# Attention stage of a two-layer trunk: causal mask by a TensorE product, one minimum and one transposed copy per pair

## The chip, the cores and the metric

The kernel runs on one core of one Trainium2 chip. The metric is the device time of one launch in microseconds, of which each kernel has several runs; a profiled execution gives the trace. TensorE multiplies matrices into PSUM (eight banks of 512 float32 per partition), VectorE, ScalarE and GpSimd (POOL in the profile) work on rows of 128 partitions, and SyncE issues transfers. Each engine works its own list of instructions in order, and engines meet by semaphores that the kernel sets and waits for by hand.

## The reference, cut to what matters

The trunk has two layers, each with a mixer (a recurrent unit, six heads of latent attention, six heads of sparse attention) and a channel mixer (dense in the first layer, eight experts in the second), on 512 tokens of 1024 numbers. The change touches attention alone. What its pairs of heads compute is a causal softmax over 512 keys (with 512 tokens the selected blocks and the window of the sparse attention are all keys up to the query):

```python
def masked_softmax(s, mask):
    s = jnp.where(mask, s, NEG_INF)
    m = jnp.max(s, axis=-1, keepdims=True)
    e = jnp.where(mask, jnp.exp(s - m), 0.0)
    return e / jnp.maximum(jnp.sum(e, axis=-1, keepdims=True), 1e-30)

        s = jnp.einsum('bqhd,bkhd->bhqk', qi, k).astype(jnp.float32) * scale
        p = masked_softmax(s, (kpos[None, :] <= qpos[:, None])[None, None])
        return jnp.einsum('bhqk,bkhd->bqhd', p.astype(v.dtype), v)
...
        out = gt[..., 0:1] * o_c + gt[..., 1:2] * o_s + gt[..., 2:3] * o_w
```

`o_c` is attention over 31 compressed keys, computed ahead of the stage; `o_s` and `o_w` are the selected and the window branch, and `gt` are the gates of a head.

## The kernel before

Per layer there is a long preparation (input projections, rotary turns, norms, written out step by step in the list `PREPARE`), then the attention stage, then the output projection and the channel mixer. The attention stage works through nine pairs of heads, `PAIRS`: six sparse ones (three pairs of heads, each for branch 1 and 2, kind `nsa`, with 64 rows of keys per head) and three latent ones (kind `mla`, 96 rows). Each pair is cut into four query blocks of 128 (`TT` = 4). One iteration g is a pair u and a block i = g mod 4, with (i + 1) x 128 keys; there are `ND` = 36 iterations. The two heads of a pair are `ab` = 0 and 1, and an item is n = 2g + ab.

The order is written by hand, as one loop per engine over g, with fixed distances:

- TensorE: `scores(g)` (two float32 products into two of four score banks; in sparse pairs the heads sit in rows 0 to 63 and 64 to 127), then `turn(g-3)` (float32 transposes of 128x128 blocks of the weights, head 0 into bank 4, head 1 into bank 5), then `values` of the pair before: for key block kb the products of all queries from block kb on. The first value step of a sparse branch 1 also multiplies the compressed weights (line 1376). In the first iterations `spare` products on the identity `identb` (line 423) fill TensorE.
- VectorE: `maximum(2g)`, `maximum(2g+1)` (line 2111: adds the mask `causal`, negates, writes the block back to PSUM and takes the minimum into `nmx`), then `scale(g-2)` (sum, for sparse pairs times the reciprocal of the gate, then reciprocal) and two `scaled` (line 2134: the weights times the factor of each row). Steps of the recurrent unit (`lru_finish`) are laid into g = 14 to 21, and `collect` takes a finished pair out of PSUM.
- ScalarE: `exps(g)` (line 1657: two exps with the sum of each row), then `turned(g-3)` (line 1668: one copy for each head of the transposed blocks to `PT_`).

So one pass of an item is: scores, maximum, exp, scaling, transposes, copy, value products. `scores` waits for the exps of two iterations back, `turn` waits for `scaled` (`pn`) and for the copy of the item two before (`pt`), which frees the turn bank.

## Time and profile before

| | us |
|---|---|
| median of three runs | 1374.83 |
| lowest, highest | 1374.44, 1375.63 |
| span of the profiled execution | 1373.5 |
| attention stage of layer 0, from 144.1 to 243.5 | 99.4 |
| attention stage of layer 1, from 765.0 to 863.2 | 98.2 |
| TensorE busy over the span | 1309.3 (95%) |
| VectorE, ScalarE busy over the span | 993.8 (72%), 686.0 (50%) |

The span runs from the first to the last instruction of one execution. A busy TensorE is not TensorE at its peak: its products are pipelined, and one record lasts longer than the distance to the next. In a list in order of time, the distance between two starts is what a block of work costs.
### The profile page before, as it was taken

What the parts mean: (1) busy time and instruction counts of PE and PEld (TensorE: products, weight loads), DVE (VectorE), ACT (ScalarE), POOL (GpSimd) and SP (SyncE); (2) the same over time, 40 slices, a digit from 0 to 9 for tenths busy, and PEclk for the clock granted to TensorE, in tenths of its full rate; (3) what the DMA queues carried; (4) which work ended last, traced back from release to release, by engine and by line L of the source; (5) the groups of instructions that cost most, each with busy time, mean ns of one, the idle gap of its engine ahead of it and who ended that gap; (6) DMA issues with size and microseconds to landing.
All of it is one profiled execution on the core that took longest, in us unless ns stands there. A gap on an engine that the chain in (4) does not pass through costs nothing.

```text
span 1373.5 us, 24997 instructions
## 1 busy us (share of the span) xinstructions
PE 1309.3 (95%) x10313; PEld 817.6 (60%) x10313; DVE 993.8 (72%) x1611; ACT 686.0 (50%) x1042; POOL 131.8 (10%) x113
## 2 busy tenths in 40 slices
PE   7999899999999999999999999989999999999992
PEld 4347445444444444444356445559988988988981
DVE  6985797686650366334895797567888889989996
ACT  5244676253320232212245776347487677677672
POOL 0010420320000000031010100320400000000003
PEclk9999999999999999999999999999999999999996
DMA  8330685324320344003331100229899999999975
GB/s 308 112 104 16 231 293 173 138 98 179 138 92 0 116 160 168 0 16 134 138 93 32 31 1 1 78 80 366 331 368 386 333 349 396 369 367 383 368 296 200
DMA packets 39998, 255.69 MB, mean 186 GB/s; under 512 B 5626, under 2 KB 6650, under 8 KB 25418
## 3 DMA queue, kind: packets, MB, share of 16 engines
q1 hardware_dynamic: 30490, 220.20, 42.6%
q0 software_dynamic: 8960, 33.26, 7.3%
q8 instruction: 84, 1.38, 0.4%
q10 hardware_dynamic: 432, 0.59, 0.1%
q14 instruction: 32, 0.26, 0.1%
HBM read 218.28 MB, written 33.65 MB: 183 GB/s over the span
## 4 chain that ended last, share of the span: by engine, by line
PE 81%; DVE 8%; issue 5%; DMA 3%; ACT 2%; POOL 1%; SPq 0%; DVEq 0%; POOLq 0%; ACTq 0%
PE bank L1120 19%; PE bank L1121 19%; PE bank L1122 19%; PE bank L1341 3%; PE bank L1387 2%; PE bank L1357 2%; DVE bank L2111 2%; DVE arena L2134 2%; PE bank L681 1%; PE bank L683 1%; PE bank L682 1%; PE bank L673 1%; PE bank L672 1%; PE bank L671 1%; DMA expert_slots<-arena,row_index 1%
## 5 line engine op out<-in xcount | busy, mean ns | idle before, releaser
L931 DVE SCALAR_TENSOR_TENSOR arena<-arena 128x3072 f16<-128x3072 f32 x86 | 288.3, 3352 | 10.8 <-ACT arena L785 10.7
L785 ACT ACTIVATE arena<-arena 128x3072 f16<-128x3072 f32 x86 | 237.9, 2767 | 41.6 <-DMA arena<-in_ew 19.9
L1120 PE MATMUL bank<-arena 128*128 128x144 bf16 (+3 forms) x894 | 219.3, 264 | 6.8 <-DVE arena L931 2.9
L1121 PE MATMUL bank<-arena 128*128 128x144 f16 (+3 forms) x894 | 219.2, 264 | 0.0
L1122 PE MATMUL bank<-arena 128*128 128x144 bf16 (+3 forms) x894 | 219.2, 264 | 0.0
L1120 PE MATMUL bank<-hh,wring_hi 128*128 128x512 bf16 x352 | 133.9, 380 | 0.0
L1122 PE MATMUL bank<-hh,wring_lo 128*128 128x512 bf16 x352 | 133.7, 380 | 0.0
L1121 PE MATMUL bank<-hl,wring_hi 128*128 128x512 f16 x352 | 133.7, 380 | 0.0
L1122 PE MATMUL bank<-hh,arena 128*128 128x512 bf16 x338 | 128.1, 379 | 0.0
L1121 PE MATMUL bank<-hl,arena 128*128 128x512 f16 x338 | 128.1, 379 | 0.0
L1120 PE MATMUL bank<-hh,arena 128*128 128x512 bf16 x338 | 128.1, 379 | 0.0
L1120 PE MATMUL bank<-wring_hi,arena 128*128 128x112 bf16 (+1 forms) x704 | 113.6, 216 | 0.6 <-DVE arena L931 0.5
L1122 PE MATMUL bank<-wring_hi,arena 128*128 128x112 bf16 (+1 forms) x704 | 113.5, 216 | 0.0
L1121 PE MATMUL bank<-wring_lo,arena 128*128 128x112 f16 (+1 forms) x704 | 113.4, 216 | 0.0
L1460 ACT ACTIVATE wring_hi<-wstage 128x1024 f16<-128x1024 f32 x44 | 46.3, 1054 | 131.2 <-PE bank L1122 124.4
L1120 PEld LDWEIGHTS bank<-arena 128*128 128x128 f16 x894 | 87.4, 98 | 32.5 <-DVE arena L931 3.5
L1657 ACT ACTIVATE arena<-bank,small 128x128 f32<-128x128 f32 (+3 forms) x144 | 75.0, 525 | 57.0 <-DVE small L2111 51.8
L1121 PEld LDWEIGHTS bank<-arena 128*128 128x128 f16 x894 | 87.5, 98 | 22.8 <-issue 0.3
L1122 PEld LDWEIGHTS bank<-arena 128*128 128x128 f16 x894 | 87.5, 98 | 22.4
L2111 DVE CUSTOM_DVE_ANT_0 bank<-bank,causal 128x128 f32<-128x128 f32 (+3 forms) x144 | 68.7, 510 | 22.0 <-PE bank L1341 21.1
L1476 ACT ACTIVATE arena<-arena 128x512 f32<-128x512 f32 x22 | 13.9, 630 | 135.1 <-DVE arena L1832 135.1
L671 PE MATMUL bank<-arena 128*128 128x144 bf16 (+2 forms) x352 | 74.2, 233 | 1.6 <-DVE arena L964 1.6
(332 smaller groups left out, 2618.3 us busy)
## 6 DMA issues: line engine op xcount, KB each, us to landing
arena<-in_ew SPq DMA_DIRECT2D x86, 1536.0 KB, 9.1
arena<-in_dw SPq DMA_DIRECT2D x22, 1536.0 KB, 6.5
wstage<-in_w_chunk SPq DMA_DIRECT2D x44, 512.0 KB, 3.6
expert_results<-iota POOLq DMA_DIRECT2D x9, 2048.0 KB, 21.3
arena<-in_cmp_w SPq DMA_DIRECT2D x2, 2048.0 KB, 10.0
expert_slots<-iota POOLq DMA_DIRECT2D x5, 512.0 KB, 18.8
expert_results<-wstage SPq DMA_DIRECT2D x5, 512.0 KB
arena<-in_w_tok SPq DMA_DIRECT2D x2, 1096.0 KB, 7.3
```

The lines of the kernel that those rows point to most:

```text
L671: pe.matmul(out, hi, a_hi, start=(first and m % 2 == 0), stop=False, skip_group_check=True)
L785: act.activation(ew_hi_[:, G % EP, :], ew[:, G % ES, :], ACT.Copy, scale=SW).then_inc(M["hi_ready"], 1)
L931: dve.scalar_tensor_tensor(out=ew_lo_[:, G % EP, :], in0=ew[:, G % ES, :], scalar=SW, in1=ew_hi_[:, G % EP, :], op0=ALU.mult, op1=ALU.subt ...
L1120: pe.matmul(out, w_hi, x_hi, start=first, stop=False)
L1121: pe.matmul(out, w_hi, x_lo, start=False, stop=False)
L1122: return pe.matmul(out, w_lo, x_hi, start=False, stop=last)
L1341: pe.matmul(score_bank[n % 4][:, 0:N], q, k, start=True, stop=True).then_inc(*signal("s_mm", l, n))
L1357: mm = pe.transpose(turn_bank[n % 2][:, at * P:(at + 1) * P], Pt[u % 2][:, ab, OFF[i] + kb * P:OFF[i] + (kb + 1) * P], ident[:, :])
L1387: mm = pe.matmul(ob[ab * HD:(ab + 1) * HD, kb * P:T], v, turned_row(u % 2, ab, kb), start=(kb == 0 and kind == "mla"), stop=(closes and kb ...
L1460: act.activation(wring_hi[:, J % WR, :, :], wstage[:, J % WS, :, :], ACT.Copy, scale=SW).then_inc(*signal("w_hi", J))
L1657: act.activation(Pt[u % 2][:, ab, OFF[i]:OFF[i] + N], score_bank[n % 4][:, 0:N], ACT.Exp, bias=nmx[:, n % 8:n % 8 + 1], scale=-1.0, accum_ ...
L2111: dve.tensor_tensor_reduce(block, block, causal[:, T - (i + 1) * P:], -1.0, 3.0e38, ALU.add, ALU.min, nmx[:, m:m + 1]).then_inc(*signal("n ...
```

## The change

The keys of the sparse pairs and the queries of the latent pairs are negated where they are scaled anyway, so a score product gives the negated scores. After the two score products of an iteration come two bf16 products of the identity `identb` with `causalb` (0 or 1e30) that add the mask to the last 128 columns of each bank; one semaphore step follows both heads. `maximum(g)` is one `tensor_reduce` with minimum over both banks, and writes nothing back. `exps(g)` waits once, for both. The factor of a row is the reciprocal of the sum alone; the gate enters as a second per-partition scalar of `scaled` for sparse pairs, and the reciprocal of all gates after the compressed probabilities goes. `turned(g)` is one copy for both heads, from banks 4 and 5; `turn(g)` waits before its first transpose for the copy of g-1. `PT_` gets a layout in which both heads have the same pattern (352 more words per partition). The mask table shrinks from 512 to 128 columns, and POOL makes a bf16 copy of it at the start.

```diff
-        causal = sb("causal", T)
+        causal = sb("causal", P)
+        causalb = sb("causalb", P // 2)[:, :].bitcast(BF16)
...
-        PT_ = arena[:, used[0]:used[0] + 2 * 2 * NP_ + T]
+        PB = 3 * (TT - 1) + TT
+        PT_at = used[0]
+        PT_ = arena[:, PT_at:PT_at + 2 * 2 * PB * P].rearrange("p (s a b c) -> p s a b c", s=2, a=2, c=P)
...
-        PROW = 5 * P
-
-        def turned_block(s, ab, i):
-
-
-
-            a = s * TT * PROW + (0 if ab == 0 else (TT - 1 - i) * PROW)
-            if ab == 0:
-                return PT_[:, a:a + TT * PROW].rearrange("p (r c) -> p r c", c=PROW)[:, 0:i + 1,
-                                                                                     (i + 1) * P:(i + 2) * P]
-            w = PROW + P
-            return PT_[:, a:a + (i + 1) * w].rearrange("p (r c) -> p r c", c=w)[:, :, 0:P]
+
+        def turned_block(s, i):
+
+            return PT_[:, s, :, i:i + 3 * i + 1:3, :]
...
+        bank = [banks[:, i, :] for i in range(8)]
         RING = 8
         score_bank = [bank[2], bank[3], bank[0], bank[1]]
-        turn_bank = [bank[4], bank[5]]
+        score_pair = [banks[:, 2:4, :], banks[:, 0:2, :]]
+        turn_bank, turn_pair = [bank[4], bank[5]], banks[:, 4:6, :]
...
                             q, k = qh[0:DQK, h, i * P:N], kh[0:DQK, h, 0:N]
-                        pe.matmul(score_bank[n % 4][:, 0:N], q, k, start=True,
-                                  stop=True).then_inc(*signal("s_mm", l, n))
+                        pe.matmul(score_bank[n % 4][:, 0:N], q, k, start=True, stop=False)
+                    for ab in range(2):
+                        mm = pe.matmul(score_bank[(2 * g + ab) % 4][:, i * P:N], identb, causalb, start=False, stop=True)
+                    mm.then_inc(*signal("s_mm", l, g))
...
                             emptied(4 + n)
-                        if n >= 2:
-                            pe.wait_ge(*ready("pt", l, n - 2))
+                        if g >= 1 and ab == 0:
+                            pe.wait_ge(*ready("pt", l, g - 1))
                         for kb in range(i + 1):
-                            at = kb if ab == 0 else i - kb
-                            mm = pe.transpose(turn_bank[n % 2][:, at * P:(at + 1) * P],
+                            mm = pe.transpose(turn_bank[n % 2][:, kb * P:(kb + 1) * P],
                                               Pt[u % 2][:, ab, OFF[i] + kb * P:OFF[i] + (kb + 1) * P],
                                               ident[:, :])
-                        mm.then_inc(*signal("pt_mm", l, n))
+                    mm.then_inc(*signal("pt_mm", l, g))
...
                     if kb == 0:
-                        pe.wait_ge(*ready("pt", l, u * ITEMS + ITEMS - 1))
+                        pe.wait_ge(*ready("pt", l, u * TT + TT - 1))
...
-                                   scale=SCALE_MLA).then_inc(*signal("uq", l, h))
+                                   scale=-SCALE_MLA).then_inc(*signal("uq", l, h))
...
@@ -1649,11 +1647,11 @@
                 def exps(g):
                     u, i = divmod(g, TT)
                     if u >= 2 and i == 0:
-                        act.wait_ge(*ready("pt_mm", l, (u - 2) * ITEMS + ITEMS - 1))
+                        act.wait_ge(*ready("pt_mm", l, (u - 2) * TT + TT - 1))
                         act.wait_ge(*ready("scale", l, (u - 2) * TT + TT - 1))
+                    act.wait_ge(*ready("nmx", l, g))
                     for ab in range(2):
                         n, N, at = 2 * g + ab, (i + 1) * P, 2 * i + ab
-                        act.wait_ge(*ready("nmx", l, n))
...
                         act.wait_ge(*ready("pv", l, u - 2))
-                    for ab in range(2):
-                        n = 2 * g + ab
-                        act.wait_ge(*ready("pt_mm", l, n))
-                        act.copy(turned_block(u % 2, ab, i),
-                                 turn_bank[n % 2][:, 0:(i + 1) * P].rearrange("p (k q) -> p k q", q=P)
-                                 ).then_inc(*signal("pt", l, n))
+                    act.wait_ge(*ready("pt_mm", l, g))
+                    act.copy(turned_block(u % 2, i),
+                             turn_pair[:, :, 0:(i + 1) * P].rearrange("p a (k q) -> p a k q", q=P)
+                             ).then_inc(*signal("pt", l, g))
...
                     dve.scalar_tensor_tensor(out=home[name](c)[p0:p0 + rows, :], in0=b[p0:p0 + rows, :],
-                                             scalar=(SCALE_NSA if name == "q" else 1.0) / (SW * SX),
+                                             scalar={"q": SCALE_NSA, "ks": -1.0, "kw": -1.0}.get(name, 1.0) / (SW * SX),
...
                                       ALU.mult).then_inc(*signal("cmp_row", "probs", l))
...
 
-                def maximum(n):
-                    i = n // 2 % TT
-                    dve.wait_ge(*ready("s_mm", l, n))
-                    m = n % 8
-                    block = score_bank[n % 4][:, 0:(i + 1) * P]
-                    dve.tensor_tensor_reduce(block, block, causal[:, T - (i + 1) * P:], -1.0, 3.0e38, ALU.add,
-                                             ALU.min, nmx[:, m:m + 1]).then_inc(*signal("nmx", l, n))
+                def maximum(g):
+                    i, m = g % TT, 2 * g % 8
+                    dve.wait_ge(*ready("s_mm", l, g))
+                    dve.tensor_reduce(nmx[:, m:m + 2], score_pair[g % 2][:, :, 0:(i + 1) * P], AX_X,
+                                      ALU.min).then_inc(*signal("nmx", l, g))
 
                 def scale(g):
 
                     u, i = divmod(g, TT)
                     kind, c, br = PAIRS[u]
-                    if g == 0:
-                        dve.wait_ge(*ready("ginv", l))
                     dve.wait_ge(*ready("p", l, 2 * g + 1))
-                    r, total = rsum[:, u % 2, 2 * i:2 * i + 2], ssum[:, u % 2, 2 * i:2 * i + 2]
-                    if kind == "nsa":
-                        link(dve.scalar_tensor_tensor(out=r, in0=total, scalar=1e-30, in1=ginv[:, i, c:c + 4:3, br],
-                                                      op0=ALU.max, op1=ALU.mult))
-                    else:
-                        link(dve.tensor_scalar(r, total, 1e-30, None, ALU.max))
-                    dve.reciprocal(r, r).then_inc(*signal("scale", l, g))
+                    dve.reciprocal(rsum[:, u % 2, 2 * i:2 * i + 2],
+                                   ssum[:, u % 2, 2 * i:2 * i + 2]).then_inc(*signal("scale", l, g))
                     dve.wait_ge(*ready("scale", l, g))
 
                 def scaled(n):
                     u, at = divmod(n, ITEMS)
                     i = at // 2
+                    kind, _, br = PAIRS[u]
                     v = Pt[u % 2][:, at % 2, OFF[i]:OFF[i] + (i + 1) * P]
-                    dve.tensor_scalar(v, v, rsum[:, u % 2, at:at + 1], None,
-                                      ALU.mult).then_inc(*signal("pn", l, n))
+                    if kind == "nsa":
+                        gate_at = 2 * P + 3 * head_of(u, at % 2) + br
+                        ins = dve.tensor_scalar(v, v, rsum[:, u % 2, at:at + 1], vtok[:, i, gate_at:gate_at + 1],
+                                                ALU.mult, ALU.mult)
+                    else:
+                        ins = dve.tensor_scalar(v, v, rsum[:, u % 2, at:at + 1], None, ALU.mult)
+                    ins.then_inc(*signal("pn", l, n))
 
...
                     if g < ND:
-                        maximum(2 * g)
-                        maximum(2 * g + 1)
+                        maximum(g)
...
+            pool.tensor_copy(causalb, causal[:, :]).then_inc(*signal("by_pool", "unit"))
...
     t["byrank"] = np.tile(np.r_[NE - 1 - e, e, CAPS, RANK_AT].astype(np.float32), (P, 1))
-    t["causal"] = np.zeros((P, T), np.float32)
-    t["causal"][:, T - P:] = np.where(r[None, :] <= r[:, None], 0.0, NEG)
+    t["causal"] = np.where(r[None, :] <= r[:, None], 0.0, MASKED).astype(np.float32)
```

On TensorE, in the second sparse pair: scores of 384 keys, the turn of four blocks, values, then scores of 512 keys and the next turn. bank0 and bank1 are score banks, bank4 and bank5 turn banks, bank7 an output bank; `p` is an exp, `pn` a scaling, `pt` a copy. Before:

```order
L1341 MATMUL bank2<-arena 128x384 [waits p]
L1341 MATMUL bank3<-arena 128x384 [waits p]
L1357 MATMUL bank4<-ident,arena 128x128 [waits pt,pn]
L1357 MATMUL bank4<-ident,arena 128x128 x3
L1357 MATMUL bank5<-ident,arena 128x128 [waits pt,pn]
L1357 MATMUL bank5<-ident,arena 128x128 x3
L1387 MATMUL bank7<-arena 64x128 x2
L1341 MATMUL bank0<-arena 128x512 [waits p]
L1341 MATMUL bank1<-arena 128x512 [waits p]
L1357 MATMUL bank4<-ident,arena 128x128 [waits pt,pn]
L1357 MATMUL bank5<-ident,arena 128x128 [waits pt,pn]
```

and now (all banks are one tensor, so their numbers are not told apart):

```order
L1338 MATMUL bank<-arena 128x384 [waits p] x2
L1340 MATMUL bank<-causalb,identb 128x128 x2
L1355 MATMUL bank<-ident,arena 128x128 [waits pt,pn]
L1355 MATMUL bank<-ident,arena 128x128 x3
L1355 MATMUL bank<-ident,arena 128x128 [waits pn]
L1355 MATMUL bank<-ident,arena 128x128 x3
L1385 MATMUL bank<-arena 64x128 x2
L1338 MATMUL bank<-arena 128x512 [waits p] x2
L1340 MATMUL bank<-causalb,identb 128x128 x2
L1355 MATMUL bank<-ident,arena 128x128 [waits pt,pn]
L1355 MATMUL bank<-ident,arena 128x128 [waits pn]
```

Each pair of scores is followed by two products on the mask, and the turn's wait for `pt` stands only on the first head and now covers both.

On VectorE, one iteration with 384 keys and the start of the next, before:

```order
L2134 TENSOR_SCALAR arena<-arena,small 128x512 [waits scale]
L2134 TENSOR_SCALAR arena<-arena,small 128x512
L2111 ISA bank2,small<-bank2,causal 128x384 [waits s_mm]
L2111 ISA small 128x1
L2111 ISA bank3,small<-bank3,causal 128x384 [waits s_mm]
L2111 ISA small 128x1
L2123 SCALAR_TENSOR_TENSOR small<-small 128x2 [waits p]
L2127 RECIPROCAL small<-small 128x2 [waits dve_chained]
L2134 TENSOR_SCALAR arena<-arena,small 128x128 [waits scale]
L2134 TENSOR_SCALAR arena<-arena,small 128x128
```

and now:

```order
L2123 TENSOR_SCALAR arena<-arena,small 128x512 [waits scale]
L2123 TENSOR_SCALAR arena<-arena,small 128x512
L2104 TENSOR_REDUCE small<-bank 128x2 [waits s_mm]
L2112 RECIPROCAL small<-small 128x2 [waits p]
L2123 TENSOR_SCALAR arena<-arena,small 128x128 [waits scale]
L2123 TENSOR_SCALAR arena<-arena,small 128x128
```

Two maxima with their reads of the accumulator became one reduction, and one of the two small operations ahead of the scaling is gone.

On ScalarE, the exps of 384 and 512 keys and the copies behind them, before:

```order
L1668 COPY arena<-bank4 128x3x128 [waits pt_mm]
L1668 COPY arena<-bank5 128x3x128 [waits pt_mm]
L1657 ACTIVATE arena,small<-bank2,small 128x384 [waits nmx]
L1657 ACTIVATE arena,small<-bank3,small 128x384 [waits nmx]
L1668 COPY arena<-bank4 128x4x128 [waits pt_mm]
L1668 COPY arena<-bank5 128x4x128 [waits pt_mm]
L1657 ACTIVATE arena,small<-bank0,small 128x512 [waits nmx]
L1657 ACTIVATE arena,small<-bank1,small 128x512 [waits nmx]
L1668 COPY arena<-bank4 128x128 [waits pt_mm,pv]
L1668 COPY arena<-bank5 128x128 [waits pt_mm]
```

and now:

```order
L1664 COPY arena<-bank 128x2x3x128 [waits pt_mm]
L1655 ACTIVATE arena,small<-bank,small 128x384 [waits nmx]
L1655 ACTIVATE arena,small<-bank,small 128x384
L1664 COPY arena<-bank 128x2x4x128 [waits pt_mm]
L1655 ACTIVATE arena,small<-bank,small 128x512 [waits nmx]
L1655 ACTIVATE arena,small<-bank,small 128x512
L1664 COPY arena<-bank 128x2x128 [waits pt_mm,pv]
```

The second exp no longer waits on its own, and one copy stands where two stood.

## Rows read from the trace of the kernel before

**Rows 1.** Busy time by stretch (start:end, length, engines with counts, clock, DMA), both stages

```profile
144.10:243.50 99.40, 90.44 (x501) 44.78 (x501) 82.62 (x310) 66.50 (x219) 21.45 (x23) 1.00 0.72 238
765.00:863.20 98.20, 90.09 (x501) 44.92 (x501) 81.03 (x311) 66.64 (x220) 3.80 (x4) 1.00 0.04 10
```

**Rows 2.** TensorE in order of time (start us, us, what), one sparse pair of heads

```profile
162.28 0.49 PE L1341 MATMUL bank<-arena 64*128 64x128 f32 x4
162.71 0.66 PE L1357 MATMUL bank<-ident,arena 128*128 128x128 f32 x4
...
166.96 1.09 PE L1357 MATMUL bank<-ident,arena 128*128 128x128 f32 x8
...
168.35 1.13 PE L1341 MATMUL bank<-arena 64*128 64x512 f32 x4
...
170.29 1.08 PE L1387 MATMUL bank<-arena 128*64 128x512 f32 x4
171.30 0.49 PE L1341 MATMUL bank<-arena 64*128 64x128 f32 x4
```

**Rows 3.** Chain of waits (start us, us, what), from 168.42 to the transposes at 172.05

```profile
168.42 1.11 PE bank L1341 x4
169.53 0.68 DVE bank L2111
...
170.30 0.67 ACT arena L1657
...
171.75 0.17 ACT arena L1668
171.91 0.14 issue
```

**Rows 4.** TensorE in order of time, the latent pairs

```profile
202.55 0.71 PE L1341 MATMUL bank<-arena 96*128 96x128 f32 x4
...
211.29 0.38 PE L1357 MATMUL bank<-ident,arena 128*128 128x128 f32 x2
211.60 1.08 PE L1387 MATMUL bank<-arena 128*64 128x512 f32 x4
...
213.36 0.63 PE L1357 MATMUL bank<-ident,arena 128*128 128x128 f32 x4
...
218.41 1.04 PE L1357 MATMUL bank<-ident,arena 128*128 128x128 f32 x8
...
221.57 0.38 PE L1357 MATMUL bank<-ident,arena 128*128 128x128 f32 x2
...
222.89 0.71 PE L1341 MATMUL bank<-arena 96*128 96x128 f32 x4
```

**Rows 5.** Chain of waits, spare products on the identity at the stage's start

```profile
145.04 1.40 PE bank L423 x6
```

**Rows 6.** TensorE in order of time, two spare products between scores and turn

```profile
156.60 0.61 PE L423 MATMUL bank<-identb 128*128 128x512 bf16 x2
157.18 1.07 PE L1357 MATMUL bank<-ident,arena 128*128 128x128 f32 x8
```

**Rows 7.** Groups by shape on VectorE, whole span (count, busy us, mean ns)

```profile
L2134 DVE TENSOR_SCALAR arena<-arena,small 128x512 f32<-128x512 f32 x36 | 16.0, 488 | 0.6
...
L1957 DVE TENSOR_SCALAR arena<-arena,pp 128x512 f32<-128x512 f32 x4 | 2.2, 547 | 0.2
...
L2060 DVE TENSOR_REDUCE small<-arena 128x24 f32<-128x744 f32 x2 | 1.9, 929 | 0.8 <-ACT arena L1598 0.8
...
L2264 DVE TENSOR_REDUCE arena<-arena 128x32 f32<-128x256 f32 x2 | 0.8, 420 | 0.1
```

**Rows 8.** The page's groups: all maxima of VectorE

```profile
L2111 DVE CUSTOM_DVE_ANT_0 bank<-bank,causal 128x128 f32<-128x128 f32 (+3 forms) x144 | 68.7, 510 | 22.0 <-PE bank L1341 21.1
```

**Rows 9.** Groups by shape on ScalarE, the stage of layer 0

```profile
L1657 ACT ACTIVATE arena<-bank,small 128x512 f32<-128x512 f32 x18 | 12.3, 686 | 4.5 <-DVE small L2111 4.1
L1657 ACT ACTIVATE arena<-bank,small 128x384 f32<-128x384 f32 x18 | 10.4, 579 | 6.4 <-DVE small L2111 6.3
```

## What the change will do to the time

> **What bounds the kernel now.** I read the busy time of the engines by stretch first, to find the change's place. It acts in two attention stages, one per layer, 99 and 98 us long [rows 1]. In both, TensorE is busy 90 us, VectorE 81 to 83, ScalarE 67: three engines hand one iteration to each other, and TensorE is closest to its limit. The rest of the program holds nothing that the change prices, so the forecast is made for one stage and doubled.
>
> Next comes TensorE's own timeline for one pair of sparse heads. An iteration on TensorE is scores(g), turn(g-3), values. Four iterations (i = 0 to 3, keys 128 to 512) make a period. From one scores block of 128 keys to the next is 171.30 - 162.28 = 9.02 us [rows 2]. The work in it: scores of i = 0, 0.43 (162.28 to 162.71); the iterations of i = 1 and 2, 4.25 (162.71 to 166.96); turn and values before i = 3, 1.39 (to 168.35), and its scores, 1.11 (chain, [rows 3]; ends in the chain lie 0.07 behind the timeline's next start); two transposes, 0.31 (211.29 to 211.60, [rows 4]); the opening value products, 1.01 (170.29 to 171.30). That is 8.50; the other 0.52 is idle, in front of transposes.
>
> The chain of waits says on whom it is idle [rows 3]. Scores of 512 keys end at 169.53; the second maximum ends 0.68 later and its exp begins at 170.30; the exps take until 171.75; ScalarE's first copy, of 128 columns, 0.17; 0.14 to reach TensorE; transposes at 172.05. So **turn(g-2) can start only after maximum(g), exps(g) and the copy of turn(g-3)**: ScalarE's copies stand behind its exps. This loop, 2.52 us long, is what the change lengthens.
>
> In the latent-attention pairs the second score product starts when the first is done, so the first maximum and exp lie under it: a period is 221.57 - 211.29 = 10.28 us with hardly an idle gap [rows 4]. There TensorE is the bound.
>
> **The change, part by part.**
>
> *Mask products.* Two bf16 products of 128 columns per iteration, 36 iterations in each layer, all on TensorE, in front of the semaphore that VectorE waits for. No row shows this pair; the nearest are the spare products on the same identity between score and turn blocks. Six of 512 columns take 1.40 us, two take 157.18 - 156.60 = 0.58 [rows 5, 6]. The slope is 0.82 / 4 = 0.205 per product, so 0.05 per 128 columns, and the remainder is 0.17 per block. The pair costs 0.10 if it streams without the block cost and 0.27 with all of it. I take **0.22**, nearer to the upper row, since it is the same switch between the same kinds of block, and the turn behind it may save a little. Bounds for the range: 0.12, and 0.35 if the block cost is paid twice.
>
> The Trainium skill (TensorE: Matmul & The Clock Gate, Back-to-back issue gap) gives 134 cycles at 128 columns; as an estimate 0.11 us for two, and the forecast would be about 1386. The Trainium skill (TensorEngine Tiling (Array Packing), Key Properties) says that changing the tiling mode drains TensorE. That speaks against this product behind the 64-row scores of the sparse pairs and not behind the 96-row ones; with 0.12 there and 0.22 elsewhere the time would be about 1389. No row of before tells the two apart.
>
> *One minimum over two banks.* Reductions of 256 and 744 elements last 0.420 and 0.929 us: 1.04 ns per element and 0.153 fixed [rows 7]. Over 1024 elements that is 1.22, over 768 0.95. The mean of one maximum is 0.510 [rows 8]; two are 1.02 against 0.153 + 640 x 1.04 ns = 0.82 for the pair, 0.2 saved for VectorE per iteration. But exp of the first head can no longer start after half of it.
>
> *Scaling.* The two-element operation goes. I take 0.06 for it, an estimate below the 0.09 that lies between the end of the second maximum and its exp (a small read and the handing on, [rows 3]). A second per-partition scalar costs 0.547 - 0.488 = 0.06 [rows 7], twice per iteration in sparse pairs. So VectorE gains 0.2 + 0.06 - 0.12 = 0.14 per iteration there in all, no more.
>
> *One copy per pair.* Exps of 384 and 512 last 0.579 and 0.686 [rows 9], 0.84 ns per column; from the 0.17 of the 128-column copy [rows 3], 256 columns come to 0.28 and 1024 to 0.92. ScalarE saves some hundredths, but both turn banks now come free together, and the first transpose waits for both.
>
> *The loop after.* After scores and mask of 512 keys: 1.22 + 0.02 (handing on) + 1.35 (two exps of 0.686, the second handed on 0.02 early) + 0.28 + 0.14 = **3.01**, against 2.52. After 384 keys: 0.95 + 0.02 + 1.14 + 0.92 + 0.14 = 3.17. TensorE's own work under them, counted from the end of the last score (0.07 later than the stream's end), is 0.31 + 1.01 + 0.43 - 0.07 = 1.68 after 512 keys and 1.39 + 1.11 - 0.07 = 2.43 after 384, and the next mask, 0.22, comes on top of both. Idle after 384: 3.17 - 2.65 = 0.52. Idle after 512: 3.01 - 1.90 - 0.52 = 0.59. The loops of 128 and 256 keys are covered (their minimum and exps are shorter by more than a microsecond).
>
> Sparse period without compressed values: 8.50 + 4 x 0.22 + 1.11 = 10.49, +1.47. With the compressed values (1.0 more on TensorE) only the first idle stays: 9.51 + 0.88 + 0.52 = 10.91. From 171.30 to 202.55, 31.25 us [rows 2, 4], lie two such and one without: 32.3, **+1.05**. Part of this stretch was bound by VectorE, which has recurrent-unit steps there, so it loses least. Latent pairs: TensorE's work under the 512-key loop is 213.36 - 211.29 = 2.07, less 0.07, plus 0.22, so 3.01 - 2.22 = 0.79 idle where there was none; after 384 keys 221.57 - 218.41 = 3.16 covers 3.17. Period 10.28 + 0.88 + 0.79 = 11.95; two are 23.9 against 222.89 - 202.55 = 20.34 [rows 4], **+3.56**. This is the largest term. The first two periods, before 162.28, have few products on TensorE: three masks before the third scores (0.66) and VectorE's saving nearly cancel against the late exps, **+0.6**. The end, after 222.89: four masks 0.88, and 0.8 as an estimate for the last exps and copies that nothing overlaps any more, **+1.7**.
>
> Sum per stage: 0.6 + 1.47 + 1.05 + 3.56 + 1.7 = 8.4; two stages **+16.7 us**. On the profiled span of 1373.5 that is 1390.2, on the median 1374.83 it is **1391.5**.
>
> *Costed at nothing.* Negated keys and queries are other constants in instructions that stay. The dropped reciprocal of the gates stood behind the operation that TensorE waits for. The smaller mask table and the POOL copy lie in the first 35 us beside other loads. Larger row of the transposed buffer: memory only. If the first or second were on a path it could be worth at most a microsecond either way.
>
> **The rivals.**
>
> *The mask streams in the shadow (0.12).* The same sum with 0.12: head 0.3, sparse 1.17 and 0.14, latent 2.96, end 1.3: 5.9 per stage, 1386.5. For it: products in a stream stand close. Against it: the 0.58 for two spares.
>
> *VectorE sets the pace, faster than before.* In the middle of the stage VectorE is full, and every iteration there is shortened by its saving. If that held in the 24 sparse iterations of each stage, with masks and late exps hidden under VectorE, it is 24 x 0.14 x 2 = 7 us, 1368. It decides if TensorE's idle before transposes was owed to VectorE, so that the longer loop has slack. For it: VectorE's 82 us. Against it: the chain through ScalarE, and latent pairs that TensorE bounds.
>
> *It comes out even.* The minimum over two banks takes half the time (0.53 less at 512 keys) and the mask 0.12. Then the loop of 512 keys is 2.48, the sparse period 9.6, the latent one 11.0, and the sum about +2: 1377. Against it: the slope of 1.04 ns in the reductions shown.
> The Trainium skill (VectorE: DVE Perf Modes, The perf-mode tier table) has the reduction at one element per cycle only, which the slope agrees with.
>
> *Heavier.* The mask costs 0.35 and the transposes wait fully for both banks: sparse +1.9 and +2.2, latent +4.3, ends +3.2: 11.6 per stage, 1398.
>
> **How the numbers follow.** Forecast, mask near 0.22: 0.50. Mask hidden, 1386.5: 0.20. Heavier, 1398: 0.12. Even, 1377: 0.08. Faster, 1368: 0.10. The range 1377 to 1399 leaves out the faster case, half of the even one and the tail of the heavier. A measurement of this kernel tells 0.2%, about 2.7 us, from no change. Faster by more 0.10, within 0.09, slower 0.81.
>
> **What would show it.** Right: a stage of 106 to 109 us; latent periods near 12 us with an idle gap of 0.7 to 0.9 before the two-block transposes, put down to ScalarE's copy; score blocks of 0.2 more; a minimum of 1.2 us at 512 keys; VectorE's busy time per stage down by a few us without use. Wrong: mask pairs that add under 0.1; a 512-key minimum near 0.7; or a transpose that mostly waits for VectorE's scaling, which would make the VectorE rival the better account.

## The result and the profile after

The changed kernel takes 1397.47 us (median of 4 runs, 1395.30 to 1397.98); the kernel before, beside it on the same chip, 1374.63 (4 runs, 1374.22 to 1375.63). The ratio is 1.0159, 95% interval 1.0145 to 1.0174: 22.8 us slower. The profiled executions last 1395.9 and 1373.5 us.

First the page of after: the span, the busy time of the engines, and the groups of minima and exps.

```profile
span 1395.9 us, 24792 instructions
PE 1319.4 (95%) x10397; PEld 826.2 (59%) x10457; DVE 976.8 (70%) x1321; ACT 680.4 (49%) x970; POOL 133.5 (10%) x114
L1655 ACT ACTIVATE arena<-bank,small 128x128 f32<-128x128 f32 (+3 forms) x144 | 74.8, 525 | 81.1 <-DVE small L2104 71.2
L2104 DVE TENSOR_REDUCE small<-bank 128x2 f32<-128x256 f32 (+1 forms) x72 | 59.3, 823 | 58.5 <-PE bank L1340 58.3
```

VectorE lost 17 us of work (993.8 before) and ScalarE 5.6, and the kernel is slower all the same. The minima take 59.3 us where the 144 maxima took 68.7 [rows 8], or 73.5 together with the small reads of the accumulator behind them, which are rows of their own. But in front of the minima VectorE is idle for 58.5 us instead of 22.0. Time moved from work into waiting.

The windows of both stages (same columns as [rows 1]), and two stretches from before the third score block of each layer:

```profile
144.10:255.50 111.40, 99.30 (x575) 50.37 (x576) 74.13 (x166) 63.94 (x183) 21.18 (x23) 0.97 0.63 211
776.30:884.00 107.70, 95.92 (x572) 48.47 (x573) 73.32 (x167) 63.98 (x184) 3.35 (x4) 1.00 0.03 8
154.00:160.00 6.00, 6.00 (x25) 3.25 (x24) 2.68 (x7) 2.71 (x9) 2.48 (x3) 0.54 1.00 311
783.00:787.00 4.00, 2.50 (x18) 1.32 (x18) 3.58 (x10) 3.33 (x11) 0.00 (x0) 1.00 0.24 46
```

I measure a stage from its first 128-key score block to the first product behind its last values, and cut it at the same blocks as the prediction. In us per stage:

| part | before | after | difference | forecast |
|---|---|---|---|---|
| first two periods (head) | 18.17 / 17.06 | 21.16 / 18.17 | +3.0 / +1.1 | +0.6 |
| sparse period without compressed values | 9.02 | 9.87 | +0.85 | +1.47 |
| three sparse periods | 31.25 | 33.88 | +2.63 | +1.05 |
| two latent periods | 20.34 | 22.63 | +2.29 | +3.56 |
| end | 18.91 | 21.44 | +2.53 | +1.7 |
| stage, layer 0 / layer 1 | 97.7 / 96.6 | 109.0 / 106.0 | +11.3 / +9.4 | +8.4 |

Where one number stands, the layers agree within 0.02. Of the difference between the spans, 22.4 us, the two stages hold 20.7. Between them nothing changed. Behind the second one the program takes 513.6 instead of 511.9 us, 1.7 more. No edit touches that part, and in the profiled executions of the eleven other kernels with a mask it takes 512.5 to 515.9 us, so these 1.7 us lie within its scatter and are not shown to belong to the change.

### The profile page after: what moved, and what is told of

Same layout as the page of the kernel before. It is cut to its first block, busy times and chain, and to the rows that moved or that the text cites. A ratio compares the mean times of both kernels' runs of the same rounds, so it can differ in the third digit from the quotient of the medians.

```text
span 1395.9 us, 24792 instructions
## 1 busy us (share of the span) xinstructions
PE 1319.4 (95%) x10397; PEld 826.2 (59%) x10457; DVE 976.8 (70%) x1321; ACT 680.4 (49%) x970; POOL 133.5 (10%) x114
## 3 DMA queue, kind: packets, MB, share of 16 engines
q8 instruction: 85, 1.39, 0.4%
## 4 chain that ended last, share of the span: by engine, by line
PE 82%; DVE 5%; issue 5%; ACT 3%; DMA 3%; POOL 1%; SPq 0%; DVEq 0%; POOLq 0%; ACTq 0%
PE bank L1117 19%; PE bank L1118 19%; PE bank L1119 18%; PE bank L1338 3%; PE bank L1355 2%; PE bank L1385 2%; DVE small L2104 2%; ACT arena L1655 2%; PE bank L678 1%; PE bank L680 1%; PE bank L679 1%; PE bank L668 1%; PE bank L670 1%; PE bank L669 1%; DMA expert_slots<-arena,row_index 1%
## 5 line engine op out<-in xcount | busy, mean ns | idle before, releaser
L1117 PE MATMUL bank<-arena 128*128 128x144 bf16 (+3 forms) x893 | 218.9, 264 | 6.4 <-DVE arena L928 3.0
L1119 PE MATMUL bank<-arena 128*128 128x144 bf16 (+3 forms) x883 | 215.0, 262 | 0.0
L1119 PE MATMUL bank<-hh,wring_lo 128*128 128x512 bf16 (+1 forms) x344 | 130.6, 380 | 0.0
L1117 PE MATMUL bank<-hh,arena 128*128 128x512 bf16 x337 | 127.7, 379 | 1.0
L1117 PE MATMUL bank<-hh,wring_hi 128*128 128x512 bf16 (+1 forms) x332 | 126.2, 380 | 0.4
L1119 PE MATMUL bank<-hh,arena 128*128 128x512 bf16 x319 | 120.9, 379 | 0.0
L1655 ACT ACTIVATE arena<-bank,small 128x128 f32<-128x128 f32 (+3 forms) x144 | 74.8, 525 | 81.1 <-DVE small L2104 71.2
L1118 PEld LDWEIGHTS bank<-arena 128*128 128x128 f16 x894 | 87.5, 98 | 22.8 <-issue 0.3
L1119 PEld LDWEIGHTS bank<-arena 128*128 128x128 f16 x894 | 87.5, 98 | 22.4
L2104 DVE TENSOR_REDUCE small<-bank 128x2 f32<-128x256 f32 (+1 forms) x72 | 59.3, 823 | 58.5 <-PE bank L1340 58.3
```

Source lines behind the costliest of these rows:

```text
L1117: pe.matmul(out, w_hi, x_hi, start=first, stop=False)
L1118: pe.matmul(out, w_hi, x_lo, start=False, stop=False)
L1119: return pe.matmul(out, w_lo, x_hi, start=False, stop=last)
L1655: act.activation(Pt[u % 2][:, ab, OFF[i]:OFF[i] + N], score_bank[n % 4][:, 0:N], ACT.Exp, bias=nmx[:, n % 8:n % 8 + 1], scale=-1.0, accum_ ...
L2104: dve.tensor_reduce(nmx[:, m:m + 2], score_pair[g % 2][:, :, 0:(i + 1) * P], AX_X, ALU.min).then_inc(*signal("nmx", l, g))
```

## What the traces show

**The loop.** The chain of waits of after, from the scores of 512 keys to the transposes of 256 keys that it holds up:

```profile
172.15 1.06 PE bank L1338 x4
173.21 0.23 PE bank L1340 x2
173.44 0.02 issue
173.46 1.24 DVE small L2104
174.70 0.02 issue
174.72 0.03 ACT arena L1655
174.75 0.56 issue
175.31 0.86 ACT arena L1655 x3
176.17 0.27 ACT arena L1664
176.44 0.14 issue
176.57 0.63 PE bank L1355 x4
```

L1340 are the mask products, L2104 the minimum, L1655 the exps, L1664 the copy, L1355 the transposes. From the end of the mask it is 0.02 + 1.24 + 0.02 + 1.45 + 0.27 + 0.14 = 3.14 us, and from the end of the scores 3.37, where [rows 3] had 2.52. The forecast said 3.01. What it missed is the exps: it took 2 x 0.686, while the chain of before already had them from 170.30 to 171.75, that is 1.45. The step between them also holds the reading of the row sums (records of 0.19 us on ScalarE behind each exp).

**Where TensorE waits for it.** TensorE in order of time, with the idle time in front and what ended it (sparse, then latent, then the end):

```profile
175.59 0.29 PE L1340 MATMUL bank<-causalb,identb 128*128 128x128 bf16 x2
176.57 0.63 PE L1355 MATMUL bank<-ident,arena 128*128 128x128 f32 x4 [0.70 <-ACT arena L1664]
...
181.99 1.07 PE L1355 MATMUL bank<-ident,arena 128*128 128x128 f32 x8 [0.83 <-ACT arena L1664]
...
219.79 0.71 PE L1338 MATMUL bank<-arena 96*128 96x128 f32 x4
220.34 0.28 PE L1340 MATMUL bank<-causalb,identb 128*128 128x128 bf16 x2
221.56 0.63 PE L1355 MATMUL bank<-ident,arena 128*128 128x128 f32 x4 [0.95 <-ACT arena L1664]
...
231.67 0.71 PE L1338 MATMUL bank<-arena 96*128 96x128 f32 x4
...
245.32 0.63 PE L1355 MATMUL bank<-ident,arena 128*128 128x128 f32 x4 [1.70 <-ACT arena L1664]
```

The gaps stand where they were expected and are put down to ScalarE's copy. From 219.79 to 231.67 a latent period takes 11.88 us, with 11.95 forecast. But the two latent periods of a stage hold only one such gap: the first, 209.04 to 219.79, is 10.75. The gap belongs to the scores of 512 keys of the period that just ended. At 209.04 those were a sparse pair's, and TensorE had the compressed values (1.0 us) to do meanwhile. The second latent period hands its gap to the end, at 233.44. The forecast charged a gap to each of the two.

**In the middle, VectorE's other steps stand in the loop.** The chain in the last (sixth) sparse pair:

```profile
201.09 0.69 DVE small L2104
201.78 0.08 DVE small L2112
...
201.89 1.02 DVE arena L2123 x2
202.91 0.59 DVE hl L2090
203.50 0.88 DVE small L2104
204.38 0.02 issue
204.40 1.24 ACT arena L1655 x4
205.64 0.91 ACT arena L1664
206.55 0.14 issue
206.69 0.41 PE bank L1355 x2
```

L2123 is the scaling of an earlier iteration, L2090 a step of the recurrent unit. Both stand in VectorE's queue ahead of the minimum, and the exps of both heads now wait behind all three. VectorE has less to do, and at 203.50 it is still late.

**The mask pair.** It begins 0.12 us ahead of what follows, behind 96-row scores and, in the sparse pairs, behind 64-row ones:

```profile
165.71 0.28 PE L1340 MATMUL bank<-causalb,identb 128*128 128x128 bf16 x2
165.83 0.61 PE L1355 MATMUL bank<-ident,arena 128*128 128x128 f32 x4
...
223.88 0.28 PE L1340 MATMUL bank<-causalb,identb 128*128 128x128 bf16 x2
224.00 0.82 PE L1355 MATMUL bank<-ident,arena 128*128 128x128 f32 x6
```

So TensorE loses 0.12 per pair, not 0.22, and the loop gets 0.23 longer (173.21 to 173.44 in the chain; behind 96-row scores the chain has 0.13). The Trainium skill (TensorE: Matmul & The Clock Gate, Back-to-back issue gap) gives 134 cycles for an isolated product of 128 columns, as an estimate 0.11 us for two, and the trace's 0.12 agrees; the same section's figure for a stream, about 81 ns each, would be 0.16 for two, which is not met here.

At the start of a stage a pair costs more. There the 64-row scores of 128 and of 256 keys follow each other, before without and now with a mask pair between them:

```profile
144.11 0.93 PE L1341 MATMUL bank<-arena 64*128 64x128 f32 x8
144.97 1.47 PE L423 MATMUL bank<-identb 128*128 128x512 bf16 x6
...
144.13 0.49 PE L1338 MATMUL bank<-arena 64*128 64x128 f32 x4
144.55 0.28 PE L1340 MATMUL bank<-causalb,identb 128*128 128x128 bf16 x2
144.77 0.70 PE L1338 MATMUL bank<-arena 64*128 64x256 f32 x4
145.41 0.28 PE L1340 MATMUL bank<-causalb,identb 128*128 128x128 bf16 x2
```

The two score blocks took 144.97 - 144.11 = 0.86 us. With the first pair they take 145.41 - 144.13 = 1.28, so this pair costs 0.42; layer 1 has the same, 0.86 and 1.27. The Trainium skill (TensorEngine Tiling (Array Packing), Key Properties) says that a change of the tiling mode drains TensorE, and the 0.42 fits that, though no run isolates it. The 0.12 elsewhere can't test it, since 64-row scores were followed by full-height products before, too.

**The head of layer 0** has TensorE at a granted clock of 0.54 from 154 to 160 us (window above); before, the same stretch had 1.00. So nearly all of it runs at the lower of the two levels, 1.2 instead of 2.4 GHz. Ahead of it stands an idle gap of 1.50 us:

```profile
150.91 0.59 PE L420 MATMUL bank<-identb 128*128 128x512 bf16 x2
153.01 1.09 PE L1355 MATMUL bank<-ident,arena 128*128 128x128 f32 x4 [1.50 <-ACT arena L1664]
...
785.19 0.63 PE L1355 MATMUL bank<-ident,arena 128*128 128x128 f32 x4 [1.50 <-ACT arena L1664]
```

The four transposes take 1.09 us there and 0.63 at the same place in layer 1, behind the same idle of 1.50 us, and there the clock stays at 1.00. The gap alone doesn't decide it. Nor is it only the changed kernel that loses the clock: of the 28 stage heads in the fourteen profiled executions, 15 have a stretch below 1.00, some of them in variants of the kernel before; the profiles of before, e4, e6 and e9 have none in their heads.

## The experiments

All parts are compared over the stretch from the third 128-key score block to the end in layer 1. In the profile of each kernel here its granted clock is 1.00. It measures 79.50 before and 87.81 after, +8.31. Times come beside the kernel before on the same chip (its medians there: 1374.63 for after, 1376.50 for e1 to e4, 1376.99 for e5, e6, e8 and e9, 1376.06 for e7, e10 and e11); where there was one run only, the stretch is the measure. The stretch itself comes from one profiled execution of each kernel.

| kernel | time | ratio to before (95%) | stretch |
|---|---|---|---|
| after | 1397.47 | 1.0159 (1.0145 to 1.0174) | 87.81 |
| e1_heads_apart | 1384.45 | 1.0053 (1.0029 to 1.0076) | 83.81 |
| e2_copies_apart | 1390.53 | 1.0096 (1.0065 to 1.0127) | 85.54 |
| e4_more_spares | 1395.00 | 1.0136 (1.0106 to 1.0166) | 87.81 |
| e5_both_apart | 1384.15 | 1.0051 (1.0032 to 1.0070) | 81.65 |
| e6_before_scaling | 1375.17 | 0.9996 (0.9983 to 1.0008) | 78.48 |
| e7_before_late_exps | 1390.52 | one run, before 1376.06 | 83.11 |
| e8_double_mask | 1405.27 | 1.0213 (1.0189 to 1.0238) | 89.91 |
| e9_interleaved | 1376.70 | 0.9998 (0.9981 to 1.0015) | 78.77 |
| e10_inter_scaling | 1372.59 | 0.9974 (0.9962 to 0.9986) | 77.71 |
| e11_tied_copies | 1382.58 | one run, before 1376.06 | 82.00 |
| e12_mask_by_head | 1381.05 | one run, before 1381.19 | 80.54 |

**A minimum and a wait per head** (the mask, the new scaling and the common copy stay):

```diff
-                    mm.then_inc(*signal("s_mm", l, g))
+                        mm.then_inc(*signal("s_mm", l, 2 * g + ab))
...
-                dve.tensor_reduce(nmx[:, m:m + 2], score_pair[g % 2][:, :, 0:(i + 1) * P], AX_X, ...)
+                for n in (2 * g, 2 * g + 1):
+                    dve.wait_ge(*ready("s_mm", l, n))
+                    dve.tensor_reduce(nmx[:, n % 8:n % 8 + 1], score_bank[n % 4][:, 0:(i + 1) * P], AX_X, ...)
...
-                    act.wait_ge(*ready("nmx", l, g))
                     for ab in range(2):
+                        act.wait_ge(*ready("nmx", l, n))
```

> The changed kernel, but with a minimum for each head again and an exp that waits for its own head alone; masks stay on TensorE. Loop theory (the exps wait for the minimum over both heads, and ScalarE's copy and TensorE's next transposes stand behind them): behind 512 keys the first exp can start 0.5 us sooner, so the idle of 0.95 us in the latent periods falls to about 0.4, the sparse periods lose about as much; 18 pairs of heads times 0.5 is 9 us, so about 1388. Mask theory (the price is the products on TensorE): nothing changes, 1396 to 1398. VectorE theory (its work sets the pace): two reductions have 0.15 us of fixed cost more per iteration, so slower, about 1400.

The stretch falls by 4.00 us, with 0.57 instead of 0.95 idle in front of the latent transposes. This is the largest single part of the loss, and the time fell below the 1388 expected.

```profile
840.15 0.63 PE L1355 MATMUL bank<-ident,arena 128*128 128x128 f32 x4 [0.57 <-ACT arena L1664]
```

**A copy per head** (the minimum over two banks stays):

```diff
-                        if g >= 1 and ab == 0:
-                            pe.wait_ge(*ready("pt", l, g - 1))
+                        if g >= 1:
+                            pe.wait_ge(*ready("pt", l, n - 2))
...
-                    act.wait_ge(*ready("pt_mm", l, g))
-                    act.copy(turned_block(u % 2, i), turn_pair[:, :, 0:(i + 1) * P] ...)
+                    for ab in range(2):
+                        act.wait_ge(*ready("pt_mm", l, 2 * g + ab))
+                        act.copy(turned_block(u % 2, i)[:, ab], turn_bank[ab][:, 0:(i + 1) * P] ...)
```

> The changed kernel, but with one copy of transposed blocks per head again, each freeing its own turn bank. Loop theory: the first transposes wait for half of a copy, at 512 keys 0.5 us sooner, at 128 keys 0.1 us sooner; what counts is the part that the idle after 512 keys does not take back, so 2 to 5 us less, about 1394. Mask theory and VectorE theory: no change, 1396 to 1398.

The stretch falls by 2.27. In this run layer 1's head, outside the stretch, ran at a clock of 0.56 from 780 to 786 us and took 20.92 us instead of 18.17, so the time hides part of the gain.

**Both apart**, the edits of the two together:

> The changed kernel with a minimum for each head and a copy for each head: mask on TensorE, gate in the scaling and the new layout stay. Loop theory: with each head handed on alone the loop is that of the kernel before plus what the mask adds; the two separate steps gave 10.9 us and 3.1 us of stage time, together 12 to 14, so 5 to 8 us over the kernel before (about 1382). If the two gains overlap (both shorten the same idle), the sum is no more than the first alone, 1385.

The stretch falls by 6.16, close to 4.00 + 2.27: the two add up. 2.15 us remain over before. By the time alone the copies seem worth nothing (1384.15 against 1384.45, on different chips). Part of that is the clock in the heads: both kernels lose it in layer 0 (0.57 from 150 to 154 us with the minima alone apart; 0.75 there and 0.88 to 160 us here), but this one also in layer 1, with 0.72 from 776 to 782 us against 1.00, and that head takes 18.63 us against 17.60. The rest of the difference is not explained.

**The waits alone, in the kernel before.** First both exps wait for the second maximum, then both copies and both transposes wait for the second head:

```diff
+                    act.wait_ge(*ready("nmx", l, 2 * g + 1))
                     for ab in range(2):
                         n, N, at = 2 * g + ab, (i + 1) * P, 2 * i + ab
-                        act.wait_ge(*ready("nmx", l, n))
```

> The kernel before with one edit: ScalarE waits for the second head's maximum before its first exp. No operation is added or moved on any engine. Loop theory: this alone costs what the pair minimum cost in the changed kernel: from the third sparse pair's first scores to the end of a stage 4.0 us more (79.5 to 83.5 in the second layer), 9 us in the whole kernel. If the loss belongs to the operations and not to the wait: no change.

```diff
-                        if n >= 2:
-                            pe.wait_ge(*ready("pt", l, n - 2))
+                        if n >= 2 and ab == 0:
+                            pe.wait_ge(*ready("pt", l, n - 1))
...
+                    act.wait_ge(*ready("pt_mm", l, 2 * g + 1))
                     for ab in range(2):
                         n = 2 * g + ab
-                        act.wait_ge(*ready("pt_mm", l, n))
```

> The kernel before with both turn banks tied: both copies wait for the transposes of both heads, and the next turn waits for both copies. Loop theory: 1 to 2.5 us more per stage over the stretch of 79.5 us, 2 to 5 in all; the changed kernel lost 2.3 in that stretch by it, there behind late exps.

+3.61 and +2.50 over before, with no instruction made longer, against 4.00 and 2.2 when they are undone in the changed kernel. The coupling of the two heads is the cost, from both sides. The total of the first, 14.5 us over before where 9 were expected, is not usable as a size: in that run layer 0 had clocks of 0.92, 0.86 and 0.88 in parts of the stage.

**The mask left out, and doubled:**

```diff
-                        pe.matmul(score_bank[n % 4][:, 0:N], q, k, start=True, stop=False)
-                    for ab in range(2):
-                        mm = pe.matmul(score_bank[(2 * g + ab) % 4][:, i * P:N], identb, causalb, ...)
+                        mm = pe.matmul(score_bank[n % 4][:, 0:N], q, k, start=True, stop=True)
```

> The changed kernel with the mask products left out; the causal mask is not applied at all, everything else is as it is. The trace of the changed kernel has 0.12 us between the start of a mask pair and the next transposes, and the minimum starts about 0.2 us later than without. Loop theory: 72 times about 0.1 to 0.2 us, so 7 to 13 us less, 1385 to 1390, still well over the kernel before. Mask theory: the whole loss goes, about 1375.

```diff
-                    for ab in range(2):
+                    for n in (0, 1, 2, 3):
-                        mm = pe.matmul(score_bank[(2 * g + ab) % 4][:, i * P:N], identb, causalb, start=False, stop=True)
+                        mm = pe.matmul(score_bank[(2 * g + n % 2) % 4][:, i * P:N], identb, causalb, start=False, stop=n > 1)
```

> The changed kernel with the mask added twice (2e30 in place of 1e30; the result is the same): two more bf16 products of 128 columns in each of the 72 iterations. Price of a mask pair by this: loop theory with the trace's distance of 0.12 us, all of it on the way in latent pairs and in the idle loop: 72 x 0.12 = 8.6 us at most, 5 to 9 expected, about 1403 beside 1396 of the changed kernel. If most of it is hidden: under 3 us.

Without the mask the total is 2974.61 us and no use: the activations differ, the routing to experts overflows, and extra rounds run behind the second stage (TensorE has 24265 records of products in all instead of 10397). The stages can be read: in layer 1 the stretch is 85.49, 2.32 below after. In layer 0 it is only 1.18 below, and nearly the whole difference is one place, where VectorE's two scalings of 512 keys take 2.17 us against 1.00 in layer 1; why isn't known. With twice the mask the stretch is 2.10 above after in both layers. Over the 28 iterations of the stretch 2.1 to 2.3 us are 0.08 us per pair, on TensorE and loop together: about a third of what the forecast took. For two layers, without the heads, that is 4.2 to 4.6 us: less than the 7 to 13 expected of the first run and near the lower end of the 5 to 9 expected of the second, whose time rose by 7.8 on another chip.

**The mask by head.** Chosen last, because the undone parts left a latent gap of 0.46 us that the kernel before doesn't have. On top of both apart, in the latent pairs, each mask product now stands behind its own score product (only this part is shown):

```diff
                         pe.matmul(score_bank[n % 4][:, 0:N], q, k, start=True, stop=False)
+                        if kind != "nsa":
+                            pe.matmul(score_bank[n % 4][:, i * P:N], identb, causalb, start=False, stop=True
+                                      ).then_inc(*signal("s_mm", l, n))
```

> The kernel after with a minimum, a wait and a transposed copy per head, and in the latent pairs each head's mask product right behind that head's score product. With the masks behind both score products, TensorE still idles 0.46 us before the two-block transposes of the second latent period, where the kernel before has no gap. Theory (the mask's place holds back the first head's minimum, which could lie under the second score product): the gaps of 0.46 go, the second latent period falls from 11.18 to 10.7 us and the stretch from the first 128-key score block of the latent pairs to the third from 21.7 to about 21.2; the time about 1382.5. Rival (a mask product between two 96-row fp32 products costs TensorE its own block cost each time, up to 0.17 us): eight pairs lose up to 1.4 us, the stretch stays at 21.7 or grows to 22.5, the time 1384 to 1386.

TensorE in order of time, the start of the second latent period:

```profile
845.37 0.22 PE L1340 MATMUL bank<-causalb,identb 128*128 128x128 bf16 x1
845.43 0.44 PE L1338 MATMUL bank<-arena 96*128 96x128 f32 x2
845.70 0.22 PE L1340 MATMUL bank<-causalb,identb 128*128 128x128 bf16 x1
845.76 0.61 PE L1358 MATMUL bank<-ident,arena 128*128 128x128 f32 x4
```

The gap is gone, and the second latent period is 10.76 us, from 11.18 (10.7 expected). The first, which had no gap, grew from 10.53 to 10.76, so a pair that is split costs 0.06 more; the two together come to 21.52, between what the theory and its rival gave. The end of the stage shrank from 19.53 to 18.58, with 0.61 instead of 1.22 idle in front of its last two-head transposes of 256 keys: the late first minimum was paid there too. The stretch falls by 1.11. The time, one run, equals the one run of before beside it (1381.05 and 1381.19), but the stretch is still 1.04 longer, and before had medians of 1374.63 to 1376.99 elsewhere; one run each doesn't show the two equal.

**The new scaling alone, in the kernel before** (reciprocal of the sums only, the gate as a second scalar):

```diff
-                        link(dve.scalar_tensor_tensor(out=r, in0=total, scalar=1e-30, in1=ginv[:, i, c:c + 4:3, br], ...))
...
-                    dve.reciprocal(r, r).then_inc(*signal("scale", l, g))
+                    dve.reciprocal(rsum[...], ssum[...]).then_inc(*signal("scale", l, g))
...
-                    dve.tensor_scalar(v, v, rsum[:, u % 2, at:at + 1], None, ALU.mult)
+                    dve.tensor_scalar(v, v, rsum[:, u % 2, at:at + 1], vtok[:, i, gate_at:gate_at + 1], ALU.mult, ALU.mult)
```

> The kernel before with the scaling of the changed one alone: the reciprocal of the sum, the gate as a second per-partition scalar, no reciprocal of the gates. VectorE has one small operation less per iteration and 0.06 us more in each of the two scalings of sparse pairs. Loop theory: VectorE is not what TensorE waits for except in the middle of the stage: within 1 us of before. VectorE theory: 0.06 us per latent iteration gained, 0.06 lost per sparse one, also within 2 us. A loss of 3 us or more would say that scaling is a part of the price.

The stretch gets 1.02 us shorter; the whole time shows no difference (0.9983 to 1.0008). VectorE's busy time falls from 993.8 to 986.9 us, of which 1.2 are the two reciprocals of the gates.

**More spare products in the head of layer 0's gap** (eight instead of two at g = 1):

```diff
-                        spare(pe, 2, out_bank[0], identb, still)
+                        spare(pe, 8 if g == 1 else 2, out_bank[0], identb, still)
```

> The changed kernel with eight instead of two spare products ahead of the second turn, where TensorE is idle for 1.5 us; 6 more products of 0.21 us. Clock theory: the low granted clock of the first stage (0.54 between 154 and 160 us) comes from that idle, and goes; 2 to 4 us less, about 1394.5. If the low clock has another cause or costs nothing there: 1396 to 1398.

The first row is the head of layer 0, the second the end of the same stage:

```profile
154.00:160.00 6.00, 5.16 (x33) 2.71 (x31) 4.90 (x10) 4.36 (x12) 2.26 (x2) 1.00 1.00 318
229.00:252.00 23.00, 19.50 (x110) 11.10 (x109) 12.89 (x31) 10.88 (x28) 0.00 (x0) 0.93 0.00 1
```

The head of layer 0 falls from 21.16 to 18.47 us and the clock there is 1.00, while layer 1's head, at full clock in both kernels, stays at 18.17 and 18.18. So the lowered clock cost 2.7 us, and the added products themselves nothing. In the same execution the end of that stage has a clock of 0.93 and is 1.1 us longer. The whole gains 2.5 us, with intervals that overlap: whether eight spares hold the clock for good isn't shown.

**Another order on ScalarE, in the kernel before.** Since the copies stand behind the exps, the first head's copy goes between the exps; then the same with the new scaling.

```diff
-                    if g < ND:
-                        exps(g)
+                    for ab in range(2):
+                        if g < ND:
+                            exps(g, ab)
+                        if g >= 3:
+                            turned(g - 3, ab)
...
-                    if g >= 3:
-                        turned(g - 3)
```

> The kernel before with one edit of ScalarE's order: exp of the first head, copy of the first head's transposed blocks, exp of the second, copy of the second, in place of both exps and then both copies. Loop theory: TensorE's idle in front of transposes is owed to copies behind exps; the first copy comes one exp sooner (0.36 to 0.69 us), so the idle of about 0.5 us in each sparse pair shrinks, 2 to 6 us less than before. VectorE theory or a bound on TensorE alone: no change. It would be slower if the second exp, now behind a copy that waits for TensorE's transposes, keeps VectorE's scaling or a score bank waiting.

> The kernel before with the two edits that shortened its stages: copies between the exps (1.5 us less over both stages) and the new scaling (2.4 us less). If they act on different waits the stages together are 3 to 4 us shorter than before, ratio 0.997; if they take the same idle, 2.4 us, ratio 0.998.

Alone, each takes a microsecond off the stretch at most (0.73 and 1.02) and nothing that the time shows; the 2 to 6 us expected of the order alone did not come. Together they take 1.79 off, so the two add up, and the time is 1372.59 (12 runs) against 1376.06 (17 runs): 0.9974, interval 0.9962 to 0.9986, as forecast for two different waits. That is 0.3% below the kernel before. Before, the chain of waits leaves TensorE in the second latent period for a maximum at 221.77; here it holds TensorE's work alone through both, of which these are three lines:

```profile
826.62 1.01 PE bank L1387 x4
827.63 0.64 PE bank L1341 x4
828.27 0.45 PE bank L1357 x4
```

## Why the prediction held, and where its sizes were off

The stretch, +8.31 us, is accounted for by one part undone after another: 4.00 for exps that wait for the minimum of both heads, 2.16 for the common copy, 1.11 for masks behind both latent scores. The 1.04 that is left fits the mask's own work, 2.1 to 2.3, less 1.02 for the scaling. That last step is arithmetic: the mask was priced in the changed kernel and the scaling in the kernel before, and what the minima without mask and writing back, or the new layout of `PT_`, do by themselves was not run.

The forecast of +16.7 us was 5.7 short of the 22.4 between the profiled spans. Of these, 2.7 are the lowered clock in layer 0, 1.7 lie behind the stages and within their scatter, and 1.3 are the two stages.

- *What bounds the kernel*: right. The loop through ScalarE's copies is what got longer, and the gaps in front of the transposes are put down to them. One line of [rows 3] was misread without harm: the maximum at 169.53 is the first head's, not the second's (its exp begins at 170.30, while VectorE works at the second from 170.12 to 170.85), and the 2.52 stand.
- *Mask pair, 0.22*: too high. It is 0.12 on TensorE, the lower bound, and 0.08 as the whole stage feels it. "The same switch between the same kinds of block" was the step that failed: the remainder of 0.17 that I took from two spares of 512 columns was not paid by this pair in the stream. Only between two blocks of 64-row scores, at a stage's start, did the pair cost more, 0.42.
- *Minimum of 1.22*: right, 1.224 at 1024 elements (0.957 at 768, forecast 0.95). So was the 0.2 saved per iteration: 73.5 less 59.3 us over 72 iterations.
- *Loop, 3.01*: measured 3.14. The exps are 1.45, not 1.35. The forecast saw the mask's 0.23 us in the loop only as work on TensorE.
- *Three sparse periods, +1.05*: the term that failed, +2.63. "So it loses least" was wrong. With the minima apart this stretch falls by 1.78, with both apart by 2.73 (the whole of it), and with the late exps alone in before it rises by 1.98. In the chain at 201.89 the minimum stands behind VectorE's other steps, and both exps wait for it; that all of the stretch goes that way is argued from it and not counted.
- *Latent pairs, +3.56*: +2.29. The period with the gap was right (11.88 against 11.95); but two gaps were counted where there is one, and each mask pair was 0.1 too dear.
- *Sparse period, +1.47*: +0.85; 0.40 of the excess is too much mask, the rest too much idle. *Head, +0.6*: at full clock +0.3 in layer 0 (18.47 in e4) and +1.1 in layer 1, about right on average although it charged three of the eight mask pairs there; and 2.7 for the lowered clock of layer 0, which the forecast didn't have at all.
- *End, +1.7*: +2.53. The gap of 1.70 in front of the last two-head transposes of 256 keys had been 0.68, and the gap of 0.94 at 233.44 is the one that the forecast had put a period earlier; latent pairs and end together were forecast at 5.3 and measured 4.8. With both apart, 0.95 us of the end come back when the mask goes behind each head's scores. The 0.8 had been an estimate.
- *Scaling*: by the forecast's prices (72 operations of 0.06 dropped, 96 second scalars of 0.06 added) VectorE would have been 1.4 us busier; alone, the edit took 6.9 us off it, 5.7 without the reciprocals of the gates. The estimate of 0.06 for the dropped operation was too low (its record lasts 0.16), and its gain shows as 1.0 us in the stretch and not in the time.

The masks that I priced too high and the coupling that I priced too low nearly cancel: +9.4 measured in layer 1, +8.4 forecast. That the sum came so near while its terms were off by up to 1.6 is in part luck. The total came out near the rival called heavier, 1398, but only half by its mechanism. The mask was cheap, and the latent part lighter even than forecast; but the wait for both banks that it stood on is real (2.2 per stretch), and its +3.2 for both ends matches the 2.8 and 3.6 measured at full clock better than the forecast's 2.3. The VectorE rival fell: its busy time went down by 17 us, and the stage did not follow.

## What to carry to other kernels

Before two operations on independent items are merged, ask who waits for the first item. Here the minima with their reads got 14.2 us shorter over both stages, and the two stretches got about 8 us longer from exps that wait for the second item and about 4.4 from the common copy. Where engines hand work round in a loop, less work on one of them is worth little unless it comes ahead of what the loop waits for (17 us less on VectorE here, and a slower kernel). The order in an engine's queue is a cheap thing to try, but alone it gave nothing here that the time shows. A forecast should count each idle gap in the period in which it falls, and take the length of a pair of operations from the chain, not from twice the mean.

## What the runs showed of the hardware

- Two bf16 products of 128 columns between fp32 blocks cost TensorE 0.12 us as a pair (start to start). In the chain the pair takes 0.23 us behind 64-row scores and 0.13 behind 96-row ones. It costs 0.42 us between two blocks of 64-row scores, and 0.18 us when they are split by an fp32 product: (10.76 - 10.06) / 4 in the latent period without a gap, against (10.53 - 10.06) / 4 = 0.12 unsplit.
- The granted clock fell to 0.54 after an idle gap of 1.50 us in one layer and stayed at 1.00 after the same gap in the other; in the kernel with a copy per head it fell in both, to 0.57 from 150 to 154 us and to 0.56 from 780 to 786, after gaps of 1.40 and 1.39 us. Of the 22.4 us between the profiled spans, 2.7 hang on that.
- The kernel without its mask took 2974.61 us, since the number of expert rounds depends on the data. A kernel that leaves out work ahead of a routing step can be read by stage only.
